# Routing: the first norm's scaling goes to ScalarE and GpSimd, transposes and router products go by column halves, a residual row moves within the first expert step

## The reference

```python
def layer_norm(x, g, b):
    xf = x.astype(jnp.float32)
    mu = jnp.mean(xf, axis=-1, keepdims=True)
    var = jnp.mean(jnp.square(xf - mu), axis=-1, keepdims=True)
    return ((xf - mu) * lax.rsqrt(var + LN_EPS) * g + b).astype(x.dtype)

def moe(h, router_w, router_b, w_up, b_up, w_down, b_down):
    ...
    logits = (xt @ router_w + router_b).astype(jnp.float32)
    top_vals, top_idx = lax.top_k(logits, TOP_K)
    gates = jax.nn.softmax(top_vals, axis=-1)
    ...
    def expert_block(args):
        xblk, e = args
        hcat = xblk @ w_up[e] + b_up[e]
        x_glu = jnp.minimum(hcat[:, 0::2], SWIGLU_LIMIT)
        x_lin = jnp.clip(hcat[:, 1::2], -SWIGLU_LIMIT, SWIGLU_LIMIT)
        act = x_glu * jax.nn.sigmoid(SWIGLU_ALPHA * x_glu) * (x_lin + 1.0)
        return act @ w_down[e] + b_down[e]
    ...

def first_block(...):
    ...
        mix = hybrid_mixer(h, w_in[l], lower_bounds[l], ...)
        h = layer_norm(DEEPNORM_ALPHA * h + mix, ln1_g[l], ln1_b[l])
        ffn = moe(h, router_w[l], router_b[l], expert_w_up[l], ...)
        h = layer_norm(DEEPNORM_ALPHA * h + ffn, ln2_g[l], ln2_b[l])
    return h
```

## Time and profile before

| | us |
|---|---|
| median of 3 runs | 1694.58 |
| lowest and highest of them | 1693.18, 1694.87 |
| the profiled execution, its own time | 1691.89 |
| its span, first to last instruction | 1690.1 |
| TensorE busy | 1649.2 (98%) |
| VectorE busy | 676.7 (40%) |
| ScalarE busy | 580.7 (34%) |
| GpSimd busy | 43.0 (3%) |

### The profile page before, as it was taken

The page is one execution under the profiler, slowest core; times in us unless marked ns, Lnnn a source line. Parts: engine busy times, 40 slices in busy tenths (PEclk is TensorE's granted clock), DMA queues, the critical chain, the costliest instruction groups (busy, mean ns, idle before and its releaser), DMA issues.

```text
span 1690.1 us, 23878 instructions
## 1 busy us (share of the span) xinstructions
PE 1649.2 (98%) x9885; PEld 1047.2 (62%) x9885; DVE 676.7 (40%) x1195; ACT 580.7 (34%) x820; POOL 43.0 (3%) x26
## 2 busy tenths in 40 slices
PE   9999999989999999999999999999999999999998
PEld 8999853333333333333333333349999989999997
DVE  4776641212121212121212121244597675666654
ACT  6655321111111111011111111144464797466433
POOL 0000000000000000000000000000100032000000
PEclk9999999999999999999999999999999999999999
DMA  8556799999999999999999999986556653555552
GB/s 269 200 199 239 293 418 426 422 410 430 431 431 432 432 431 432 431 432 431 431 430 431 430 431 430 431 311 184 180 178 222 186 172 126 177 184 184 188 188 87
DMA packets 145732, 539.45 MB, mean 319 GB/s; under 512 B 8226, under 2 KB 102878, under 8 KB 120702
## 3 DMA queue, kind: packets, MB, share of 16 engines
q1 hardware_dynamic: 143310, 534.20, 79.9%
q10 hardware_dynamic: 2352, 4.23, 0.9%
HBM read 537.33 MB, written 1.08 MB: 319 GB/s over the span
## 4 chain that ended last, share of the span: by engine, by line
PE 64%; DMA 12%; DVE 2%; ACT 2%; issue 1%; SPq 0%
PE bank L1501 17%; PE bank L175 10%; PE bank L177 10%; PE bank L176 9%; PE bank L1536 9%; DMA expert_weights<-in_expert_w_up_dram 6%; DMA expert_weights_late<-in_expert_w_up_dram 6%; PE bank L1476 2%; PE bank L1457 2%; PE bank L1521 2%; PE bank L1465 1%; ACT back_w_hi L119 1%; DVE back_w_lo L123 0%; PE bank L1470 0%; PE bank L2132 0%
## 5 line engine op out<-in xcount | busy, mean ns | idle before, releaser
L1394 DVE TENSOR_TENSOR pre_act<-bank,bias_now 128x512 f32<-128x512 f32 x64 | 44.0, 688 | 648.9 <-PE bank L1521 648.9
L123 DVE TENSOR_TENSOR back_w_lo<-raw_weights,back_w_hi 128x2048 fp32r<-128x2048 f32 x90 | 205.6, 2287 | 91.6 <-ACT back_w_hi L119 90.6
L1501 PE MATMUL bank<-expert_weights_late,x_gathered 128*64 128x512 f32 x1008 | 222.5, 593 | 9.4 <-DMA expert_weights_late<-in_expert_w_up_dram 9.4
L175 PE MATMUL bank<-u_hi,back_w_hi 128*128 128x256 f32 x704 | 201.2, 286 | 0.2 <-DVE u_lo L1939 0.2
L119 ACT ACTIVATE back_w_hi<-raw_weights 128x2048 fp32r<-128x2048 f32 x90 | 170.2, 1892 | 89.9 <-PE bank L177 89.6
L176 PE MATMUL bank<-u_lo,back_w_hi 128*128 128x256 f32 x704 | 199.1, 283 | 0.0
L177 PE MATMUL bank<-u_hi,back_w_lo 128*128 128x256 f32 x704 | 199.1, 283 | 0.0
L1501 PE MATMUL bank<-expert_weights,x_gathered 128*64 128x512 f32 x752 | 166.7, 593 | 7.8 <-DMA expert_weights<-in_expert_w_up_dram 7.8
L1501 PEld LDWEIGHTS bank<-expert_weights_late,x_gathered 128*64 128x64 f32 x1008 | 71.3, 137 | 157.1 <-issue 135.7
L1315 ACT ACTIVATE pre_act<-bank 128x512 f32<-128x512 f32 x32 | 19.1, 597 | 392.9 <-PE bank L1501 379.8
L175 PEld LDWEIGHTS bank<-u_hi,back_w_hi 128*128 128x128 f32 x704 | 134.9, 192 | 2.8 <-issue 2.6
(11 more groups left out here) (422 smaller groups left out, 2643.3 us busy)
## 6 DMA issues: line engine op xcount, KB each, us to landing
expert_weights_late<-in_expert_w_up_dram SPq DMA_DIRECT2D x63, 2048.0 KB, 23.8
expert_weights<-in_expert_w_up_dram SPq DMA_DIRECT2D x47, 2048.0 KB, 24.5
expert_weights_late<-in_expert_w_down_dram SPq DMA_DIRECT2D x31, 2048.0 KB, 28.0
raw_weights<-in_w_in_dram SPq DMA_DIRECT2D x55, 1024.0 KB, 5.4
expert_weights<-in_expert_w_down_dram SPq DMA_DIRECT2D x22, 2048.0 KB, 28.0
raw_weights<-in_expert_w_up_dram SPq DMA_DIRECT2D x15, 2048.0 KB, 23.0
raw_weights<-in_w_up_dram SPq DMA_DIRECT2D x22, 1024.0 KB, 5.0
raw_weights<-in_expert_w_down_dram SPq DMA_DIRECT2D x8, 2048.0 KB, 26.9
```

The source lines that it names most:

```text
L123: dve.tensor_tensor(self.w_lo[:, s, 0:size], self.s.raw[:, s, 0:size], self.w_hi[:, s, 0:size].bitcast(FP32), ALU.subtract).then_inc(self. ...
L175: pe.matmul(out, lhsT=ah, rhs=bh, start=start, stop=False, skip_group_check=shared)
L1394: dve.tensor_tensor(both.rearrange("p g k n -> p (g k) n").rearrange("p a (h n) -> p a h n", h=2), TB[b][:, :].rearrange("p (a h n) -> p a ...
L1501: m = pe.matmul(up_out_rows(b, half), lhsT=xg[:, 2 * u + a, :], rhs=w[:, a, b, half, :, :], start=(first and a == 0), stop=(last and a == 1))
```

## The change

There are three edits.

1. The norm's scaling, one VectorE instruction for each tile, becomes a copy with a scale on ScalarE (`scale_rows`) and an addition of b on GpSimd, both in place on `s.h`. VectorE's `scaled_rows` is gone, and `top_mask` waits for the inverse deviation itself.
2. `centred` counts halves of 512 columns. TensorE's transposes and router products are written by halves `c` (tile `c // 2`, half `c % 2`) and interleaved; the two clock-keeping products are gone.
3. In the first expert step `residual_row(1, 1)` stands behind the down products.

```diff
@@ -240,7 +240,7 @@
         for c, x in enumerate(sources):
             ins = self.dve.scalar_tensor_tensor(out=self.h[:, t, n * c:n * c + n], in0=x, scalar=self.mv[:, t, 0:1],
                                                 in1=self.g[:, n * c:n * c + n], op0=ALU.subtract, op1=ALU.mult)
-            if centred is not None and c == len(sources) - 1:
+            if centred is not None:
                 ins.then_inc(centred, 1)
             else:
                 self.own.add(ins)
@@ -472,6 +472,11 @@
             for t in range(TT):
                 pool.memset(score[:, 2 * t, :, :], 0.0).then_inc(levels_zero, 1)
 
+            pool.wait_ge(ln_loaded, 32)
+            for t in range(TT):
+                pool.wait_ge(rows_scaled, t + 1)
+                pool.tensor_tensor(s.h[:, t, :], s.h[:, t, :], ln_b, ALU.add).then_inc(h_ready, 1)
+
         def scalar(act):
             own = Count(act, act_own)
 
@@ -600,13 +605,30 @@
             split_hi(act, NW + 6)
             split_hi(act, NW + 7)
             act.preload_act_table_set(LOG_EXP)
-            for t in range(TT):
+
+            def row_root(t):
                 act.wait_ge(var_ready, t + 1)
                 inverse_root(act, own, mv[:, t, 3:4], mv[:, t, 2:3], mv[:, t, 1:2], 1.0, s.eps_ln, ln_rstd)
-                for c in range(2 * t, 2 * t + 2):
-                    act.wait_ge(ht_mm, c + 1)
-                    act.activation(hT[:, 4 * (c % 2):4 * (c % 2) + 4, P * t:P * t + P],
-                                   s.bank[HT_BANK[c]][:, :].rearrange("p (k t) -> p k t", k=4), ACT.Copy).then_inc(ht_out, 1)
+
+            def turned_copy(c):
+                t = c // 2
+                act.wait_ge(ht_mm, c + 1)
+                act.activation(hT[:, 4 * (c % 2):4 * (c % 2) + 4, P * t:P * t + P],
+                               s.bank[HT_BANK[c]][:, :].rearrange("p (k t) -> p k t", k=4), ACT.Copy).then_inc(ht_out, 1)
+
+            def scale_rows(t):
+                act.wait_ge(ln_rstd, t + 1)
+                act.wait_ge(ht_mm, 2 * t + 2)
+                act.activation(s.h[:, t, :], s.h[:, t, :], ACT.Copy, scale=mv[:, t, 3:4]).then_inc(rows_scaled, 1)
+
+            row_root(0)
+            turned_copy(0)
+            turned_copy(1)
+            scale_rows(0)
+            turned_copy(2)
+            row_root(1)
+            turned_copy(3)
+            scale_rows(1)
             for t in range(TT):
                 act.wait_ge(top_ready, t + 1)
                 act.activation(rt[:, t, 0, :], lg[:, t, :], ACT.Exp, bias=cnt[:, t:t + 1]).then_inc(ex_ready, 1)
@@ -843,15 +865,11 @@
                     dve.wait_ge(ln_loaded, 32)
                 norm.centre(t, [s.h[:, t, 0:512], s.bank[2 + t][:, :]], centred)
 
-            def scaled_rows(t):
-                dve.wait_ge(centred, t + 1)
-                dve.wait_ge(ht_mm, 2 * t + 2)
-                norm.scale(t)
-
             def top_mask(t):
 
                 dve.wait_ge(lg_mm, t + 1)
                 dve.wait_ge(rb_ready, 1)
+                dve.wait_ge(ln_rstd, t + 1)
                 thr, ge, eq, rank, mask = top[:, t, TOP_K - 1:TOP_K], rt[:, t, 2, :], rt[:, t, 3, :], rt[:, t, 4, :], rt[:, t, 1, :]
                 sync_step(dve.scalar_tensor_tensor(out=lg[:, t, :], in0=s.bank[t][:, 0:N_EXPERTS], scalar=mv[:, t, 3:4], in1=router_bias[:, :],
                                                    op0=ALU.mult, op1=ALU.add))
@@ -881,9 +899,7 @@
             centred_rows(0)
             dve.wait_ge(st.gemm_done, NW + 12)
             centred_rows(1)
-            scaled_rows(0)
             top_mask(0)
-            scaled_rows(1)
             top_mask(1)
             for t in range(TT):
                 first_slots(t)
@@ -1143,34 +1159,29 @@
 
             pe.wait_ge(bias_ready, 4)
 
-            def keep_clock(n, bank):
-
-                for i in range(n):
-                    pe.matmul(s.bank[bank][:, 0:256], lhsT=C("identity"), rhs=s.con[:, 1:3, :].rearrange("p n c -> p (n c)"), start=True, stop=True)
-
-
-            def turned_rows(t):
-                pe.wait_ge(centred, t + 1)
-                for c in range(2 * t, 2 * t + 2):
-                    for i in range(4):
-                        k = 4 * (c % 2) + i
-                        m = pe.transpose(s.bank[HT_BANK[c]][:, P * i:P * i + P], s.h[:, t, k * P:k * P + P], C("identity"))
-                    m.then_inc(ht_mm, 1)
-
-            def router(t):
-                for k in range(KD):
-                    if k % 4 == 0:
-                        pe.wait_ge(ht_out, 2 * t + k // 4 + 1)
+            def turned_half(c):
+                pe.wait_ge(centred, c + 1)
+                for i in range(4):
+                    k = 4 * (c % 2) + i
+                    m = pe.transpose(s.bank[HT_BANK[c]][:, P * i:P * i + P], s.h[:, c // 2, k * P:k * P + P], C("identity"))
+                m.then_inc(ht_mm, 1)
+
+            def router_half(c):
+                t = c // 2
+                pe.wait_ge(ht_out, c + 1)
+                for k in range(4 * (c % 2), 4 * (c % 2) + 4):
                     m = pe.matmul(s.bank[t][:, 0:N_EXPERTS], lhsT=hT[:, k, t * P:t * P + P], rhs=rw[:, k, :], start=(k == 0), stop=(k == KD - 1))
-                m.then_inc(lg_mm, 1)
-
-            turned_rows(0)
-            keep_clock(1, 7)
-            router(0)
+                return m
+
+            turned_half(0)
+            turned_half(1)
+            router_half(0)
             pe.wait_ge(rb_ready, 1)
-            turned_rows(1)
-            keep_clock(1, SPARE)
-            router(1)
+            turned_half(2)
+            router_half(1).then_inc(lg_mm, 1)
+            turned_half(3)
+            router_half(2)
+            router_half(3).then_inc(lg_mm, 1)
             pe.wait_ge(h_ready, 1)
             s.residual_row(pe, 0, 0)
             m0, m1 = rt[:, 0, 1, :], rt[:, 1, 1, :]
@@ -1589,9 +1600,7 @@
                 pe.wait_ge(bank_t_read, i * 2 + 1)
                 if not last:
                     gather(i + 1)
-                if known and r == 0:
-                    s.residual_row(pe, 1, 1)
-                else:
+                if not (known and r == 0):
                     for t in range(TT):
                         scatter_rows(t)
                 if known and r == GATE_STEP:
@@ -1607,6 +1616,8 @@
                     unit_loaded(q, j + 4 + b, place[4 + b], after)
                     pe.wait_ge(act_ready, i * 2 + b + 1)
                     down_part(j + 4 + b, place[4 + b], b, after, last)
+                if known and r == 0:
+                    s.residual_row(pe, 1, 1)
 
             if first:
                 pe.wait_ge(s.first_onehot, 2)
```

4 lines of the change are left out of this document (2 added, 2 removed).

## The result

| | before | after |
|---|---|---|
| median | 1693.26 (7 runs) | 1699.66 (7 runs) |
| lowest and highest | 1692.21, 1694.87 | 1698.07, 1701.1 |
| profiled execution | 1691.89 | 1700.95 |

The ratio is 1.0033, 95% interval [1.0024, 1.0043], so the change makes the kernel slower by 5.6 us (4.1 to 7.3; 0.0033 x 1693.3 and so on). I had forecast 1697.5, "within 0.2%" as the likeliest outcome, and a range up to 1699.6, which the median misses by 0.06 us. The sign of the shift was right, its size was not: slower by over 0.2% is what came, and it had only 0.25. The forecast was built on a median of 1694.58, which with more executions became 1693.26. On that base the likeliest case (+2.9) is 1696.2, 3.5 us too low, and the case of the falling clock is 1697.4 to 1697.9: so the measured time lies above every case that I had.

A forecast was written before the change was run, and what follows sets the result against it. Taken as bound by weight transfers at 431 GB/s, with TensorE's lateness passed on fully: 2.35 + 0.57 = 2.9 us on the profiled 1691.89 gives 1694.8, and the median 2.7 above gives 1697.5; range 1693.3 to 1699.6.

The forecast's parts named there:

- the likeliest case: The forecast itself: VectorE's selection in the routing held, +2.35 us, and first expert step, +0.57; 2.9 us slower, chance 0.36.
- the case of the falling clock: Routing: TensorE's wait lowers its clock, 1.2 to 1.75 us on top of 2.9, for 1698.7 to 1699.3; chance 0.18.
- Factor 1, the last dip: Expert stage: TensorE's lateness at the first step reaches the last transfer dip, at 373 us, and the end in full.
- TensorE's order and ScalarE: Routing: tile 0's products end at 217.97, tile 1's at 220.22; ScalarE's scalings of 1152 ns each add no term.
- GpSimd's additions: Routing: each addition of b takes 2.4 us, bounds 2.39 and 4.7; the adds as such hold nobody.
- What the additions do to VectorE: Routing: additions hold VectorE's two-input and tensor-scalar selection instructions; TensorE starts on tile 1's mask at 225.4, +2.35 us.
- my second rival: Routing: only two-input VectorE instructions wait; shift +1.7 or +0.7 before the first expert step's 0.57; 1695.9 to 1696.9, chance 0.24.
- Step 0: First expert step: with the residual row moved, TensorE waits for ScalarE's copy of the gathered rows; +0.57 us, bounds 0 to 0.6.
- the third rival: Routing: the clock falls while TensorE waits about 2.4 us for tile 0's mask; 1698.7 to 1699.3, chance 0.18.
- My first rival: Routing: small VectorE instructions slip past GpSimd's additions; -0.66 us there, -0.1 with the first expert step; 1694.5, chance 0.18.

The follow-up runs named there:

- the order alone: Kernel before with only TensorE's transposes and router products by halves, no clock-keeping products; 1693.34, ratio 1.0002.
- the residual row alone: Kernel before with only residual_row(1, 1) moved behind the down products of the first expert step; 1694.62, ratio 1.0007.
- without the additions: Changed kernel with GpSimd's two additions of b left out, so its output differs from the reference; 1694.32, ratio 1.0000.
- with four clock-keeping products: Changed kernel with four clock-keeping products between the first residual row and the first product on tile 0's mask; 1696.51, ratio 1.0017.
- the held selection with five: Changed kernel without GpSimd's additions, VectorE's first selection instruction of tile 0 issued 13 times, five clock-keeping products in TensorE's wait; 1696.57, ratio 1.0016.
- the scaling alone: Kernel before with only the norm's scaling moved to ScalarE and GpSimd, TensorE's order and clock-keeping products kept; 1700.79, ratio 1.0048.
- the held selection: Changed kernel without GpSimd's additions, VectorE's first selection instruction of tile 0 issued 13 times instead of once; 1701.35, ratio 1.005.

## Why the prediction was right, and where it failed

**Factor 1, the last dip: right within the spread, and helped by luck at the dip itself.** The lateness found at the first expert step (7.36) is close to that of the batch at the dip (7.2), but only because two falls of the clock in between nearly cancel. The better evidence is the set of runs. The lateness of the load behind step 0 (at 265.32 before) and the measured time are 0.1 and 0.3 us for the order alone, 0.9 and 1.2 for the residual row alone, 0.1 and 0.0 without the additions, 2.7 and 2.9 with four clock-keeping products, 3.2 and 2.7 for the held selection with five, 6.8 and 8.1 for the scaling alone, 5.9 and 8.5 for the held selection. (The row that the prediction calls the last of the earlier trace rows is its first.)

**TensorE's order and ScalarE: right.** Tile 0's first product stands at 216.64 - 215.36 = 1.28 us behind the first transpose (forecast 1.33), the two scalings took 1.15 and 1.14 us (forecast 1.152), and the second addition was asked for at 221.22 - 1.12 = 220.10, as written.

**GpSimd's additions: right,** 2.35 and 2.34 for 2.4. SyncE's load behind h_ready went from 221.10 to 222.47 with the offset taken out (forecast 222.5).

**What the additions do to VectorE: the mechanism was right, +2.35 was +1.77.** The tensor-scalar comparison does wait, as taken from the earlier trace rows, and one instruction of VectorE lasts over 2 us. That it is one with two inputs would have been so under my second rival as well; the 1.10 us of the comparison tell the two apart. The mis-sized piece is "the scan would be at 220.2. GpSimd's second add is asked for at 220.1 and goes first". VectorE was a little ahead: scan and count slipped in, and the product L885 was held instead, so the mask was done 0.40 us behind the second addition and not 0.88.

**Step 0: +0.57 measured +0.85.** The turning of the gathered rows starts 0.77 us behind that of the scatter matrix against 0.22 before, a wait of 0.55; turning, down products and the residual row behind them took 0.3 us more than in the old order.

**The step that failed** is the one on which the likeliest case was built without a term for TensorE's clock. I had the mechanism as the third rival, with 0.18, for "the wait is shorter than 4.43 us and residual rows lie around it". Both were true and neither helped: 1.83 us of waiting between light products was enough. The earlier trace rows showed a fall behind a wait of 4.43 us, and I read it as if shorter waits were safe. And the rival's price was too low. I took 1.75 us, the loss of one group of 16 products. The low clock lasted 10 us and cost 4.74, because it covered the mask's products, a residual row, the gathering and the up products. "1698.7 to 1699.3" was therefore the sum of an overpriced selection (2.9 for 2.62, with step 0) and an underpriced clock. The Trainium skill, "TensorE: Matmul & The Clock Gate", section "Terms", has the price as the time spent at the lower level times one half; over the 10 us here that gives an estimate of 5 us, and the trace (4.74) agrees. I should have priced a fall by its length, and not by one group of products.

My first rival, that small instructions slip past, and the second, that only two-input instructions wait, are both refuted by the 1.10 us of the comparison in after and the 1.49 us in the scaling alone. The Trainium skill, "SBUF — State Buffer", section "Who interferes with whom", which I leaned on, has the tensor-scalar right beside the two-input addition. It also says that a two-input VectorE instruction contends with a GpSimd instruction that reads SBUF, and there the measurement differs: L885 took 0.19 us beside a one-input GpSimd instruction, 2.23 beside a two-input one. The tensor-scalar comparison, too, took its usual 0.24 us beside the one-input instruction (0.50 for tile 1).

## What to carry to other kernels

Before you give an elementwise tensor-tensor operation to an idle GpSimd, look at what VectorE does meanwhile: a chain of eleven 0.2 us instructions on the critical path is the worst neighbour, since any of those that take part in the conflict can be held until GpSimd's instruction ends. When an edit makes TensorE wait between light products, give the wait two prices, its own and that of a lowered clock on everything behind it, and fill it with idle products if it can't be removed: here four (or two) of them gave back half of the loss. Here clock-keeping products helped in the place where TensorE would stand, and not ahead of the router products. And before you read a cost of 1 or 2 us from the lateness at one point of two traces, look for falls of the clock in between that only one of them has.
